# Gates of two dense tiles: built with one-hot matmuls, or added into zeroed memory by indirect transfers

## What is computed

```
scores = einsum(q, sub_keys)              # 8 heads, 2 halves of 128 keys
sv, si = top_k(scores, 16)                # for each half
cand   = sv[0][:, None] + sv[1][None, :]  # 256 candidates
top_s, pos = top_k(cand, 16)
idx  = 128 * si[0][..] + si[1][..]        # an expert of 16384
gate = softmax(top_s)                     # 8 heads x 16 = 128 pairs (idx, gate) a token
a    = expert_u[idx] . x
out  = sum(gate * gelu(a) * expert_v[idx])
```

## Time and profile before

| | us |
|---|---|
| median of 3 runs | 1688.26 (1687.2 to 1694.93) |
| profiled execution, its own time | 1689.51 |
| its span, first to last instruction | 1687.8 |
| mean granted TensorE clock | 0.982 |
| before the first dense stage | 0 to 495 |
| first dense stage | 495 to 1145 |
| second dense stage | 1145 to 1670 |
| end | 1670 to 1688 |

### The profile page before, as it was taken

How to read it: one execution, slowest core, us unless ns; L and a number is a source line. 1 busy time by engine, 2 the same in 40 slices (tenths; PEclk the granted TensorE clock), 3 DMA queues, 4 the chain that set the end, 5 groups by cost and what they waited for, 6 DMA issues and landing times.

```text
span 1687.8 us, 22615 instructions
## 1 busy us (share of the span) xinstructions
PE 1587.2 (94%) x7605; PEld 1292.7 (77%) x7605; DVE 1258.3 (75%) x2268; ACT 664.9 (39%) x1227; POOL 391.9 (23%) x326
## 2 busy tenths in 40 slices
PE   1899988999999999999989999799999999999995
PEld 0454465554559999999989999798888888888884
DVE  6448364439957987899788988558888878788887
ACT  2111132221337852588336853233333333333333
POOL 1101400000002320033001346413344334334420
PEclk9989989999999999999999999999999999999998
DMA  9765420000127994489736999987999999999982
GB/s 361 275 229 181 149 76 0 1 0 1 50 85 278 363 360 150 160 325 357 278 135 224 361 387 413 402 314 261 367 352 345 354 357 354 329 362 359 344 315 87
DMA packets 172770, 426.26 MB, mean 253 GB/s; under 512 B 13068, under 2 KB 62220, under 8 KB 169496
## 3 DMA queue, kind: packets, MB, share of 16 engines
q1 hardware_dynamic: 86400, 265.89, 42.2%
q0 software_dynamic: 36864, 134.23, 21.8%
q10 hardware_dynamic: 49432, 25.19, 5.3%
HBM read 372.84 MB, written 52.43 MB: 252 GB/s over the span
## 4 chain that ended last, share of the span: by engine, by line
PE 87%; DVE 6%; DMA 3%; ACT 2%; issue 1%; ACTq 1%; SPq 0%; DVEq 0%
PE bank L1152 10%; PE bank L1153 10%; PE bank L1156 10%; PE bank L1097 10%; PE bank L1099 10%; PE bank L1098 10%; PE bank L1043 7%; PE bank L951 5%; PE bank L1112 5%; PE bank L1026 3%; PE bank L961 3%; PE bank L921 1%; DMA weights<-in_w_ada 1%; PE bank L1053 1%; ACTq L842 1%
## 5 line engine op out<-in xcount | busy, mean ns | idle before, releaser
L1097 PE MATMUL bank<-h_hi,u_hi 128*128 128x384 f32 x1024 | 350.7, 343 | 22.0 <-DVE u_lo L1490 13.2
L1098 PE MATMUL bank<-h_lo,u_hi 128*128 128x384 f32 x1024 | 345.0, 337 | 0.0
L1099 PE MATMUL bank<-h_hi,u_lo 128*128 128x384 f32 x1024 | 345.0, 337 | 0.0
L1152 PE MATMUL bank<-v_hi,w_hi 128*128 128x512 f32 x768 | 299.2, 390 | 1.7 <-DVE w_lo L1597 1.6
L1153 PE MATMUL bank<-v_lo,w_hi 128*128 128x512 f32 x768 | 298.8, 389 | 0.0
L865 ACT ACTIVATE v_hi<-weights 128x1024 fp32r<-128x1024 f32 x128 | 135.8, 1061 | 330.2 <-PE bank L1156 264.3
L1156 PE MATMUL bank<-v_hi,w_lo 128*128 128x512 f32 x768 | 236.4, 389 | 0.0
L1593 DVE TENSOR_TENSOR v_lo<-weights,v_hi 128x1024 fp32r<-128x1024 f32 x128 | 157.7, 1232 | 95.2 <-ACT v_hi L865 93.0
L1490 DVE TENSOR_TENSOR u_lo<-weights,u_hi 128x1024 fp32r<-128x1024 f32 x128 | 155.9, 1223 | 95.8 <-PE bank L1099 72.7
L1097 PEld LDWEIGHTS bank<-h_hi,u_hi 128*128 128x128 f32 x1024 | 194.7, 190 | 25.3 <-DVE u_lo L1490 12.8
L1098 PEld LDWEIGHTS bank<-h_lo,u_hi 128*128 128x128 f32 x1024 | 194.8, 190 | 0.0
(11 more groups left out here) (233 smaller groups left out, 2179.6 us busy)
## 6 DMA issues: line engine op xcount, KB each, us to landing
weights<-in_uT SPq DMA_DIRECT2D x128, 512.0 KB
weights<-in_expert_v SPq DMA_DIRECT2D x128, 512.0 KB, 7.8
weights<-in_w_ada SPq DMA_DIRECT2D x12, 2048.0 KB, 10.3
gates_dense<-weights SPq DMA_DIRECT2D x24, 1024.0 KB
weights<-gates_dense ACTq DMA_DIRECT2D x16, 1536.0 KB
shared<-gelu_dense SPq DMA_DIRECT2D x64, 384.0 KB, 8.9
gelu_dense<-weights SPq DMA_DIRECT2D x32, 384.0 KB
gelu_dense<-ada SPq DMA_DIRECT2D x32, 384.0 KB
```

Of the source, the lines that this page charges most:

```text
L1097: nc.tensor.matmul(a, uh[:, k, :], h2_hi[:, :, k, :], start=(k == 0), stop=False)
L1098: nc.tensor.matmul(a, uh[:, k, :], h2_lo[:, :, k, :], start=False, stop=False)
L1099: ins = nc.tensor.matmul(a, ul[:, k, :], h2_hi[:, :, k, :], start=False, stop=(k == KC - 1))
L1152: nc.tensor.matmul(acc, wh, v_hi[:, r % 2, cols], start=begin, stop=False)
```

## The change

Tiles 1 and 2 (`SCATTERED` = 2) no longer have a turn and half-groups. Their 16 groups of `g_dram` are filled with zeroes by 16 stores of SP, whose source is `gate_sparse`, set to zero by GpSimd at the start; `gates(0)` waits until these stores have ended. `gates(1)` and `gates(2)` write the gates into a block of `turned`, and three further VectorE instructions compute for each of the 128 selections its element in `g_dram`. GpSimd then adds the gates into the table: one indirect transfer for each selection k, 128 tokens of one 4-byte element each, with addition. As two heads of a token may have chosen the same expert, each head's 16 transfers wait until those of the head before have landed. The scatters of both tiles stand on GpSimd's queue behind the first eight gathers and ahead of the ninth.

Only tile 3 is built with matmuls (`BUILT` = 1). The 32 products that stood beside the half-groups of tiles 1 and 2 move into the loop (`LOOP_AT` = 8), where each has two dots; the dots beside half-groups fall from 84 to 28. The last dots are done in I = 14. ACT's copy of the turned block of tile 3 waits for the 128 scatters of tile 1, whose memory it takes, and the first `load_g` waits for all of them.

```diff
+SCATTERED = 2
+BUILT = DENSE - SCATTERED
-LOOP_AT = 12
+LOOP_AT = 8
-DOTS_IN_CHUNKS = DENSE * CHUNKS // 2 * sum(DOTS_BESIDE)
+DOTS_IN_CHUNKS = BUILT * CHUNKS // 2 * sum(DOTS_BESIDE)
...
+        g_places = g_dram.rearrange("g p n -> (g p n)").rearrange("(n a) -> n a", a=1)
+        sent_gate, sent_place = [[turned[:, d % 2, c] for d in range(SCATTERED)] for c in range(2)]
...
             sp.dma_start(keysT, sub_keysT).then_inc(keys_in, 16)
+            sp.wait_ge(zeros_made, 1)
+            for g in range(SCATTERED * CHUNKS):
+                sp.dma_start(g_dram[g].rearrange("p (a n) -> p a n", n=NSEL),
+                             gate_sparse[:, :].unsqueeze(1).broadcast_to([P, NKEYS * GROUP // NSEL, NSEL])).then_inc(g_zeroed, 16)
...
+            nc.gpsimd.memset(gate_sparse[:, :], 0.0).then_inc(zeros_made, 1)
+            nc.gpsimd.iota(token_u, [[1, 1]], base=0, channel_multiplier=1).then_inc(token_made, 1)
...
-                                wait_full(pool, "turn", 0)
+                                pool.wait_ge(places_ready, 1)
...
+                def scatter(d, h):
+                    if h == 0:
+                        pool.wait_ge(places_ready, d + 1)
+                    if d == 0 and h == 0:
+                        pool.wait_ge(g_zeroed, 16 * SCATTERED * CHUNKS)
+                    else:
+                        pool.wait_ge(scattered, 16 * TOPK * (d * PH + h))
+                    for k in range(h * TOPK, (h + 1) * TOPK):
+                        nc.gpsimd.indirect_dma_start(g_places, bass.IndirectOffsetOnAxis(sent_place[d][:, k:k + 1], 0),
+                                                     sent_gate[d][:, k:k + 1], None, compute_op=ALU.add).then_inc(scattered, 16)
+
                 one_round(0, 0, True)
+                for d in range(0 if which else SCATTERED):
+                    for h in range(PH):
+                        scatter(d, h)
                 one_round(0, 1, False)
...
-                if d >= 2:
-                    act.wait_ge(hot_gated, (d - 1) * P // HTOK)
+                if d >= 2 and d - 2 < SCATTERED:
+                    act.wait_ge(scattered, 16 * NSEL * (d - 1))
...
-            act.wait_ge(built, DTOK // BATCH)
+            act.wait_ge(scattered, 16 * NSEL * SCATTERED)
+            act.wait_ge(built, BUILT * P // BATCH)
...
+                if n == 0:
+                    dve.wait_ge(g_zeroed, 16 * SCATTERED * CHUNKS)
+                into = gate_sparse[:, :] if n == 0 else sent_gate[n - 1] if n <= SCATTERED else gate[:, :]
...
+                if 0 < n <= SCATTERED:
+                    sel_i, sel_j = picks(n)[2:4]
+                    link(stt(out=sel_j, in0=sel_j, scalar=float(NKEYS), in1=sel_i, op0=ALU.mult, op1=ALU.add))
+                    if n > 1:
+                        link(ts(token_place, token_place, float(CHUNKS * P * NKEYS * GROUP), None, ALU.add))
+                    ts(sent_place[n - 1], sel_j, float(GROUP), token_place, ALU.mult, ALU.add).then_inc(places_ready, 1)
...
+            dve.wait_ge(token_made, 1)
+            link(nc.vector.tensor_copy(token_place, token_u))
+            link(ts(token_u, token_u, GROUP - 1, None, ALU.bitwise_and))
+            link(nc.vector.tensor_copy(token_low, token_u))
+            link(tt(token_place, token_place, token_low, ALU.subtract))
+            link(stt(out=token_place, in0=token_place, scalar=float(P * NKEYS), in1=token_low, op0=ALU.mult, op1=ALU.add))
```

More of the change, by code:

```diff
@@ L133, in plan_banks @@
         jobs += query_jobs(n, QUERY_PAIRS[0]) + query_jobs(n, QUERY_PAIRS[1])
-    jobs += [(("turn", d), 5) for d in range(DENSE)]
+    jobs += [(("turn", d), 5) for d in range(SCATTERED, DENSE)]
     place, count = {}, [0] * 8
@@ L272, in program @@
         turned = ada[:, 2 * D:2 * D + 6 * P].rearrange("p (b c t) -> p b c t", b=2, c=3)
+        sent_gate, sent_place = [[turned[:, d % 2, c] for d in range(SCATTERED)] for c in range(2)]
+        sent_place = [p.bitcast(U32) for p in sent_place]
+        token_place = misc[:, 96:97]
+        token_low, token_u = misc[:, 97:98], misc[:, 98:99].bitcast(U32)
         iota128 = ada[:, 2 * D + 6 * P:2 * D + 7 * P]
@@ L333, in program @@
         gates_ready, iota_made = sem("gates_ready"), sem("iota_made")
+        zeros_made, g_zeroed, token_made = sem("zeros_made"), sem("g_zeroed"), sem("token_made")
+        places_ready, scattered = sem("places_ready"), sem("scattered")
         hot_made, hot_gated, built = sem("hot_made"), sem("hot_gated"), sem("built")
@@ L460, in _ @@
                     m += 1
-                for c in range(CHUNKS):
+                for c in range(CHUNKS if n > SCATTERED else 0):
                     for h in range(HALVES):
@@ L464, in _ @@
                         m += 1
-                    g = (n - 1) * CHUNKS + c
+                    g = (n - 1 - SCATTERED) * CHUNKS + c
                     sp.wait_ge(build_read, (g + 1) * GROUP // BATCH)
-                    sp.dma_start(g_dram[g], staging[g % 2].rearrange("p i t -> p (i t)")).then_inc(g_stored[g % 2], 16)
+                    sp.dma_start(g_dram[SCATTERED * CHUNKS + g], staging[g % 2].rearrange("p i t -> p (i t)")).then_inc(g_stored[g % 2], 16)
             def loop_product(I, r, more):
@@ L783, in gate_rows @@
                     rows = hot_i[:, half % HALVES, q, :]
-                    ins = nc.scalar.activation(rows, rows, ACT.Copy, scale=turned[:, half * HTOK // P % 2, 2, token:token + 1])
+                    ins = nc.scalar.activation(rows, rows, ACT.Copy,
+                                               scale=turned[:, (SCATTERED + half * HTOK // P) % 2, 2, token:token + 1])
                 ins.then_inc(hot_gated, 1)
@@ L807, in _ @@
                         gate_exps(n)
-                for _ in range(BEFORE_TURN):
+                for _ in range(BEFORE_TURN if d >= SCATTERED else BEFORE_TURN + AFTER_TURN):
                     product(m)
                     m += 1
+                if d < SCATTERED:
+                    continue
+                e = d - SCATTERED
                 b = wait_full(act, "turn", d)
-                if d >= 2:
-                    act.wait_ge(hot_gated, (d - 1) * P // HTOK)
+                if d >= 2 and d - 2 < SCATTERED:
+                    act.wait_ge(scattered, 16 * NSEL * (d - 1))
+                elif d >= 2:
+                    act.wait_ge(hot_gated, (e - 1) * P // HTOK)
                 release(nc.scalar.activation(turned[:, d % 2], b[:, 0:3 * P].rearrange("p (c t) -> p c t", c=3), ACT.Copy), "turn", d)
@@ L816, in _ @@
                 m += 1
-                gate_rows(d * P // HTOK)
+                gate_rows(e * P // HTOK)
                 product(m)
                 m += 1
-                gate_rows(d * P // HTOK + 1)
-                for h in range(HALVES * d * CHUNKS, HALVES * (d + 1) * CHUNKS):
+                gate_rows(e * P // HTOK + 1)
+                for h in range(HALVES * e * CHUNKS, HALVES * (e + 1) * CHUNKS):
                     copy_built(2 * h)
@@ L826, in _ @@
                     m += 1
-                    if h + HALVES < HALVES * (d + 1) * CHUNKS:
+                    if h + HALVES < HALVES * (e + 1) * CHUNKS:
                         gate_rows(h + HALVES)
@@ L848, in _ @@
             for b in range(2):
-                act.wait_ge(g_stored[b], 16 * GROUPS // 2)
-            act.wait_ge(built, DTOK // BATCH)
+                act.wait_ge(g_stored[b], 16 * BUILT * CHUNKS // 2)
+            act.wait_ge(scattered, 16 * NSEL * SCATTERED)
+            act.wait_ge(built, BUILT * P // BATCH)
             for r in range(BODY):
@@ L1124, in _ @@
                     m += 1
-                pe.wait_ge(gates_ready, d + 1)
+                if d < SCATTERED:
+                    for _ in range(AFTER_TURN):
+                        product(m)
+                        m += 1
+                    continue
+                e = d - SCATTERED
+                pe.wait_ge(gates_ready, e + 1)
                 transposes(("turn", d), [picks(n)[2], picks(n)[3], gate[:, :]])
@@ L1129, in _ @@
                     m += 1
-                if d == 0:
+                if e == 0:
                     for t in range(NT):
@@ L1159, in _ @@
             wait_read(pe, "turn", DENSE - 1)
-            pe.wait_ge(build_read, DTOK // BATCH)
+            pe.wait_ge(build_read, BUILT * P // BATCH)
             for r in range(BODY):
@@ L1398, in retrieve @@
                 yield
-                if n >= 2:
+                if n - 2 >= SCATTERED:
                     wait_full(dve, "turn", n - 2)
@@ L1462, in gates @@
                 link(nc.vector.reciprocal(gate_sum, gate_sum))
-                into = (gate if n else gate_sparse)[:, :].rearrange("p (h k) -> p h k", h=PH)
+                if n == 0:
+                    dve.wait_ge(g_zeroed, 16 * SCATTERED * CHUNKS)
+                into = gate_sparse[:, :] if n == 0 else sent_gate[n - 1] if n <= SCATTERED else gate[:, :]
+                into = into.rearrange("p (h k) -> p h k", h=PH)
```

(22 more changed lines are left out.)

## The result

1947.58 us, median of 4 runs (1944.07 to 1951.24), against 1689.52 for the kernel before on the same chip: ratio 1.1527, 95% interval 1.1503 to 1.155. The change makes the kernel 258 us slower. Forecast was 1833, slower, range 1690 to 2050. The profiled execution took 1947.36 us for a span of 1945.6.

What follows compares the result with a forecast made beforehand. TensorE, 87% of the chain, was taken as the bound, with scatters ahead of gather 8 delaying dot 8. Dot 8 at 942 + 752 tail + 133 moved products + 4 loop + 2 clock = 1833 us; range 1690 to 2050.

Steps and rivals of the forecast that it cites:

- ACT's wait: ACT's copy of tile 3's turned block waits for tile 1's 128 scatters: 728 us, where ready at about 716.
- 256 p: GpSimd's 256 scatters at p each from issue to issue: 256 x 1.48 = 379 us.
- L: Landing time of one scatter, waited for between heads on GpSimd's queue: taken 2.7 us, 16 of them 43 us.
- the prediction's own formula: Time of dot 8 in VectorE's queue, held by gather 8: 519.6 + 256 p + 16 L, forecast 942 us.
- rival B: Transfers, not GpSimd's issue, set the scatters' pace: 2105 us; chance 0.26 with everything above 1920.
- What goes: 32 of 48 builds in the first dense stage, with their DVE, ACT and store work: 46 to 62 us, taken 55.
- small costs: Small costs set against the gain of 55 us: 7 us, giving 1640 if dot 8 would not wait.
- Start and tail: First scatter on GpSimd's queue at about 517.3 us; from dot 8 to the end about 891 us.
- The loop term: Loop near the DMA's limit: each product falls behind by 0.13 us, 4 us over the 32 moved products.
- p: One scatter on GpSimd from issue to issue, bounded by gathers: taken 1.48 us, floor 0.94.
- Rival A: Scatters so cheap that the wait at dot 8 is smaller than the gain: below 1680 us, chance 0.10.
- turning point of 0.91: Scatter time from issue to issue at which wait and gain cancel, with landings of 2.7 us.
- Rival C: GpSimd loses to VectorE at nearly every issue, 2.27 us a scatter: 1877 us; within the 0.60 for 1700 to 1920.

Runs made afterwards that it cites:

- experiment 2: Changed kernel with the turned block of tile 3 in memory of its own, so ACT's copy waits for no scatter: 1945.95 us.
- Experiment 1: Changed kernel without the 256 scatters and the two waits for them; zero stores, places and order stay: 1632.66 us.
- experiment 3: Changed kernel with the same 256 scatters as plain writes, without the addition: 1902.81 us.
- experiment 4: Changed kernel with 64 of the 128 tokens in each scatter, addition kept, same number of instructions and waits: 1907.36 us.

## Why the prediction was right, and where it was short

The direction and the mechanism were right: the queue ahead of gather 8 holds dot 8, dot 8 holds `u_lo`, and that holds the core, with ACT's wait as a part of the same end (experiment 2). With the measured times in place of 256 p (424.9 of instructions and 81.8 of gaps) and of L the prediction's own formula gives dot 8 at 519.6 + 506.7 + 16 x 1.99 = 1058 us, where it is at 1058.9. The size was short by 115 us. The result lies outside the forecast's own range, 1774 to 1900; it lies inside 1690 to 2050 because that range was stretched for rival B, which did not come about. That part is luck.

- **What goes.** 55 us was taken for the builds and 7 of small costs set against it, which made 1640 without a wait. Experiment 1 gives 1632.7. Dot 8 unhindered is at 742.8, forecast 757 "up to 8 earlier", so 14 earlier; that this is the missing backlog of builds fits, but no run separates it.
- **Start and tail.** The first scatter was forecast for 517.3 and is at 517.31, which is partly luck: gather 4 starts at 511.76 and not 509.7, and gathers 4 to 7 take 5.3 us and not 7.6. The tail behind dot 8 was forecast as 891 and is 886.7. The loop term (4 us) fits: 38 products from 1132.67 to 1293.09 take 4.22 each, against 4.16.
- **L.** Taken 2.7. The 15 waits between heads are 29.8 us, 1.99 each, 11 us less in all. The Trainium skill's 2.0 us (DMA: Bandwidth & Descriptors, Anatomy of one DMA) agrees with them.
- **p, the term that failed.** "I take 1.48": the measured instruction has a mean of 1.66, with its gap 1.96. From the first scatter to the end of the last are 536 us, where 379 + 15 x 2.7 = 419 were forecast. The 117 us are the whole of the difference of dot 8 (1058.9 for 942), and with it the 115 by which the time was missed. Of them 256 x (1.66 - 1.18) = 123 are the instruction, 5 the gaps, and -11 the landings. The longer p also made ACT's wait 89.8 us, forecast 12 (728 for 716), and so two holes of the one that was forecast. The gather was a bad neighbour row: the floor of an adding scatter is 1.56 and not 0.94, of which experiment 3 gives 0.59 to the addition, and experiment 4 shows it mostly fixed. The company of VectorE, which I had given 0.24 a piece, was sized well where there was any: the scatters from 517 to 703 us, with VectorE at work, have a mean of 1.77, 0.21 over the floor. Over all 256 it is only 0.10, because more than half of them fell into the holes, where VectorE stood still (GpSimd's scatters alone, then clock, DMA share and GB/s):

```profile
517.30:703.30 186.00, 149.08 (x84) 0.98 0.67 167
...
850.00:1053.50 203.50, 160.74 (x103) 0.50 0.21 0
```

- **Rival A** (cheap scatters) falls by the same rows; even a plain write is 0.97 with a gap of 0.30, over the turning point of 0.91, and the gap of 0.30 stays without the grant.
- **Rival B** (the transfers set the pace) did not come about: the gaps between heads are 2 us and not longer, and the DMA share with nothing but scatters is 0.22. **Rival C** (GpSimd loses to VectorE) came nearer with 1877, but by the wrong route: it took 2.27 before dot 8 is due and 1.25 after, where the runs show 1.77 with a gap of 0.30 beside VectorE and 1.56 with a gap of 0.30 alone.
- The rule of the Trainium skill on writes below 512 B (DMA: Bandwidth & Descriptors, Specifications) named a cost that no row here separates. Where small writes did hurt, in experiment 3, it was not by their own time, as GpSimd went on at its pace; PE was slow, and ACT and VectorE went on late behind it.

## What to carry to other kernels

Work moved from a matrix engine to GpSimd's transfers is paid in instructions, not in bytes: count them, price one with the same operation (an addition is not a plain gather), once with the engines beside it idle and once at work (1.56 and 1.77 us here), and compare the sum with the idle time that the queue has before its next needed item. An in-order queue makes everything behind such a block as late as the block's end, so it is cut up and put where nothing is due; here two tiles in one block lose 258 us, one tile in one block 120, and one tile spread so gains 19. And look for two waits that end with the same thing before removing one of them.

## What the runs showed that was not expected

Indirect writes of 128 single elements, without addition, slowed the whole core: 11 GB/s and 21 matmuls in 51 us, and ACT and VectorE went on only 61 us behind a product's last matmul. The same number of writes of 64 elements in the same 87 us did not, nor did writes of 128 with addition, of which there were fewer. From 522 to 609 us the three runs have 63, 63 and 40 such instructions, which is 93, 46 and 59 elements per us. Whether it is the rate of small writes, and at what point it sets in, was not tried further and stays open. So does why PE's matmuls came slowly and their end was seen late; the profile puts these waits down to nothing on the core, and the load looked at above moved within 3.2 us of its issue.
